# Attention with the values standing and Pool scaling the probabilities, and new orders at four borders of a two-layer trunk

## The reference, cut to what matters

```
for l in (0, 1):
    hn = rms_norm(x)                               # x: 256 tokens x 1024, float32
    qa, ka, va, cq, ckv, kr, gates = split(hn @ w_in[l])
    # branch A: 8 heads of 64, q and k normed and rotated, causal softmax
    # branch B: 8 heads, q = rms_norm(cq) @ w_uq, (k, v) = rms_norm(ckv) @ w_ukv,
    #           q and k of 96 per head, v of 64, normed and rotated, causal softmax
    y  = softmax(q k^T * scale + mask) v           # per head, both branches
    x += (sigmoid(g_a) * (ya @ w_br_a) + sigmoid(g_b) * (yb @ w_br_b)) @ w_out
    h  = rms_norm(x)
    x += swiglu(h) if l == 0 else the two best of 8 swiglu experts per token
```

## Time and profile before

| | |
|---|---|
| Median of 3 runs | 1358.72 us (1358.40 to 1359.19) |
| The profiled execution's own time | 1360.55 us |
| Its span | 1358.7 us |
| Mean granted clock of PE | 0.995 |
| PE busy | 1340.4 us, 99% |
| DVE busy | 1036.9 us, 76% |
| ACT busy | 891.0 us, 66% |
| POOL busy | 84.6 us, 6% |
| DMA, mean | 281 GB/s |

### The profile page before, as it was taken

The page is one execution under the profiler, slowest core; times in us unless marked ns, Lnnn a source line. Parts: engine busy times, 40 slices in busy tenths (PEclk is TensorE's granted clock), DMA queues, the critical chain, the costliest instruction groups (busy, mean ns, idle before and its releaser), DMA issues.

```text
span 1358.7 us, 17852 instructions
## 1 busy us (share of the span) xinstructions
PE 1340.4 (99%) x6433; PEld 1114.4 (82%) x6433; DVE 1036.9 (76%) x946; ACT 891.0 (66%) x931; POOL 84.6 (6%) x67
## 2 busy tenths in 40 slices
PE   9999999999999999999999999999999999999997
PEld 7878888888888788888888888888888888888885
DVE  5786665544467866679899898898898998988984
ACT  6675745444365766457787687787776876877773
POOL 1220000000003200000000000000000000000000
PEclk9999999999999999989999999999999999999999
DMA  7633446555456334679999999999999999999992
GB/s 269 215 94 125 155 160 215 184 188 175 150 162 220 120 116 148 243 277 391 367 361 383 367 379 390 368 383 391 375 382 388 365 382 368 382 393 360 383 391 63
DMA packets 172905, 381.22 MB, mean 281 GB/s; under 512 B 9098, under 2 KB 29236, under 8 KB 172852
## 3 DMA queue, kind: packets, MB, share of 16 engines
q1 hardware_dynamic: 169760, 369.95, 75.5%
q0 software_dynamic: 2304, 8.39, 2.4%
q10 hardware_dynamic: 788, 2.18, 0.4%
HBM read 374.20 MB, written 6.29 MB: 280 GB/s over the span
## 4 chain that ended last, share of the span: by engine, by line
PE 91%; DVE 4%; ACT 3%; issue 1%; DMA 1%; DVEq 0%; POOLq 0%; ACTq 0%
PE ps L1122 18%; PE ps L1124 18%; PE ps L1123 18%; PE ps L692 10%; PE ps L694 10%; PE ps L693 10%; PE ps L1188 1%; ACT w_hi L1307 1%; DMA raw<-in_w_in_dram 1%; ACT mix L1297 1%; DVE w_lo L1674 1%; PE ps L1203 1%; PE ps L811 1%; DVE mix L1709 1%; DVE mix L1712 1%
## 5 line engine op out<-in xcount | busy, mean ns | idle before, releaser
L1924 DVE TENSOR_TENSOR w_lo<-mix,w_hi 128x2048 fp32r<-128x2048 f32 (+1 forms) x192 | 408.2, 2150 | 68.0 <-ACT w_hi L1528 66.4
L1528 ACT CAST w_hi<-mix 128x2048 fp32r<-128x2048 f32 (+1 forms) x190 | 341.0, 1810 | 90.1 <-PE ps L1124 90.1
L1674 DVE TENSOR_TENSOR w_lo<-raw,w_hi 128x2048 fp32r<-128x2048 f32 (+3 forms) x94 | 198.5, 2118 | 108.8 <-ACT w_hi L1307 108.1
L1122 PE MATMUL ps<-w_hi,eT_hi 128*128 128x512 f32 x704 | 278.9, 396 | 1.6 <-DVE eT_lo L2058 1.6
L1124 PE MATMUL ps<-w_hi,eT_lo 128*128 128x512 f32 x704 | 274.4, 390 | 0.0
L1123 PE MATMUL ps<-w_lo,eT_hi 128*128 128x512 f32 x704 | 274.4, 390 | 0.0
L1307 ACT CAST w_hi<-raw 128x2048 fp32r<-128x2048 f32 (+3 forms) x94 | 166.4, 1777 | 139.8 <-PE ps L694 116.8
L1924 DVE TENSOR_TENSOR w_lo<-raw,w_hi 128x2048 fp32r<-128x2048 f32 (+1 forms) x96 | 193.2, 2032 | 17.0 <-ACT w_hi L1528 16.1
L1528 ACT CAST w_hi<-raw 128x2048 fp32r<-128x2048 f32 (+1 forms) x96 | 163.3, 1711 | 48.1 <-PE ps L1124 44.4
L692 PE MATMUL ps<-w_hi,hT_hi 128*128 128x512 f32 (+1 forms) x464 | 180.2, 388 | 2.0 <-DVE w_lo L1674 2.0
L694 PE MATMUL ps<-w_hi,hT_lo 128*128 128x512 f32 (+1 forms) x464 | 177.2, 382 | 0.0
(11 more groups left out here) (208 smaller groups left out, 1520.4 us busy)
## 6 DMA issues: line engine op xcount, KB each, us to landing
mix<-in_expert_w_gate_up_dram SPq DMA_DIRECT2D x111, 1024.0 KB, 10.4
raw<-in_expert_w_gate_up_dram SPq DMA_DIRECT2D x49, 1024.0 KB, 9.1
mix<-in_expert_w_down_dram SPq DMA_DIRECT2D x48, 1024.0 KB, 11.4
raw<-in_w_in_dram SPq DMA_DIRECT2D x28, 1024.0 KB, 5.3
raw<-in_expert_w_down_dram SPq DMA_DIRECT2D x24, 1024.0 KB, 13.2
raw<-in_dense_w_gate_up_dram SPq DMA_DIRECT2D x20, 1024.0 KB, 5.1
mix<-in_expert_w_down_dram SPq DMA_DIRECT2D x25, 512.0 KB, 7.8
raw<-in_dense_w_down_dram SPq DMA_DIRECT2D x9, 1024.0 KB, 4.8
```

Of the source, the lines that this page charges most:

```text
L1122: pe.matmul(out_, l_hi, w_hi[q][:, cols], start=first, stop=False, skip_group_check=True)
L1528: act.copy(w_hi[q][:, 0:m], e_raw[raw_of(p, first)][:, 0:m]).then_inc(e_hi_ready, 1)
L1674: dve.tensor_tensor(w_lo[q][:, 0:m], raw[u % RAW][:, 0:m], w_hi[q][:, 0:m].bitcast(F32), ALU.subtract).then_inc(split, 1)
L1924: dve.tensor_tensor(w_lo[q][:, 0:m], e_raw[raw_][:, 0:m], w_hi[q][:, 0:m].bitcast(F32), ALU.subtract).then_inc(e_split, 1)
```

## The change

It makes these changes:

- `values` is issued for two heads at every odd k. v stands in the array (64 columns) and the transposed probabilities move (256 columns for the first key tile, 128 for the second). The even head's result goes to partitions 0 to 63 and the odd head's to 64 to 127, so y comes out transposed. `turn_y` and `take_y` go. ACT and DVE make `yT` hi and lo from PSUM per four heads, hi at k = 4, 8, 12 and after the loop.
- The division by the row sum is now before the turning: Pool raises the two row sums to the power -1 and multiplies the probabilities in place (`scale_probs`), and `turn_probs` waits for it. Heads 0 to 2 come before Pool's last head scales, the others after.
- ACT's weight splits in the loop move from odd k to even k, behind `turn_b`'s copy; DVE's seventh `lo` stays, its fifth moves from score 13 to score 12.
- Start: the gain vector of the attention norm is loaded by Pool's queue and no more by ACT's; `hT` is split in two halves, and the first weight unit too, so that PE starts on the first half.
- ACT splits unit u0 + 15 after the copies of the transposed q and k.
- Dense end: DVE adds the first token tile's result to x in halves, the first one before its last `lo` of the stage.
- Routing: 8 filler products and no more 12 before the ranks, none and no more 14 after them; the gather goes to four banks in four groups; ACT's fourth expert split comes after the gather's scaling.

The diff, cut to its core:

```diff
             for t_, lo, hi in ... (low, PE)
-                        if t == 0:
+                        if t == 0 and u:
                             ready(u)
-                        for t_, lo, hi in ((cq, 0, Q_RANK), (ckv, Q_RANK, LOW)):
-                            for kk in range(2):
+                        for kk in range(2):
+                            if t == 0 and u == 0:
+                                pe.wait_ge((first_split, split)[kk], 1)
+                            for t_, lo, hi in ((cq, 0, Q_RANK), (ckv, Q_RANK, LOW)):
...
                 def turn_probs(k):
-                    pe.wait_ge(exp_done, 16 * l + k + 1)
+                    pe.wait_ge(probs_scaled, 16 * l + k + 1)
...
                 def values(k):
-                    vv = v[:, k // HEADS, :, (k % HEADS) * A_DIM:(k % HEADS + 1) * A_DIM]
-                    pe.matmul(bank[:, o0:o0 + A_DIM], pT[:, k % 2, 0:P], vv[:, 0, :], start=True, stop=True)
-                    pe.matmul(bank[:, o1:o1 + A_DIM], pT[:, k % 2, P:2 * P], vv[:, 0, :], start=True, stop=False)
-                    last = pe.matmul(bank[:, o1:o1 + A_DIM], pT[:, k % 2, 2 * P:3 * P], vv[:, 1, :], start=False, stop=True)
+                    def of(hd):
+                        rows_ = slice(hd % 2 * A_DIM, (hd % 2 + 1) * A_DIM)
+                        vv = v[:, hd // HEADS, :, (hd % HEADS) * A_DIM:(hd % HEADS + 1) * A_DIM]
+                        return ps[t_.bank][rows_, (hd // 2 % 2) * T:(hd // 2 % 2 + 1) * T], vv
+                    for hd in heads:
+                        out_, vv = of(hd)
+                        pe.matmul(out_, vv[:, 0, :], pT[:, hd % 2, 0:2 * P], start=True, stop=False, skip_group_check=True)
+                    for hd in heads:
+                        out_, vv = of(hd)
+                        last = pe.matmul(out_[:, P:T], vv[:, 1, :], pT[:, hd % 2, 2 * P:3 * P], start=False, stop=True,
+                                         skip_group_check=True)
...
-                    values(k)
-                    if k == 12:
-                        turn_y(0)
+                    if k % 2:
+                        values(k)
                 branch(0, 0, 0)
-                turn_y(1)
...
-                for _ in range(12):
+                for _ in range(8):
                     pe.matmul(ps[1][:, 0:2 * P], before, both, start=True, stop=True)
...
-                for _ in range(14):
-                    pe.matmul(ps[1][:, 0:2 * P], before, both, start=True, stop=True)
...
             ACT, mixer
-                    hi(u0 + 14 + half)
+                    if half == 0:
+                        hi(u0 + 14)
                 for hp in range(4):
                     copy_out(qkT_a[:, hp, :], t_, ps[t_.bank][:, :])
+                hi(u0 + 15)
...
-                    if k % 2:
-                        g = k // 2
-                        if g < 7:
-                            hi(u0 + 17 + g)
                     if k in B_TURNS:
                         copy_out(qkT_b[0:B_DIM, hd, :], t_, ps[t_.bank][0:B_DIM, :])
-                    if k == 12:
-                        turned_y(l, 0)
+                    if k and k % 2 == 0:
+                        hi(u0 + 16 + k // 2)
+                    if k and k % 4 == 0:
+                        turned_y(l, k // 4 - 1)
...
             DVE, mixer
-                splits = {5: 16, 7: 17, 9: 18, 11: 19, 13: 20, 14: 21, 15: 22}
+                splits = {5: 16, 7: 17, 9: 18, 11: 19, 12: 20, 14: 21, 15: 22}
                     if k >= 6 and (k - 6) % 4 == 0:
-                        take_y((k - 6) // 4)
-                take_y(3)
+                        yT_low((k - 6) // 4)
                 lo(u0 + 23)
-                yT_low(1)
+                yT_low(3)
                 lo(u0 + 24)
...
             DVE, dense
+                    if u == U["dn", FF - 1, 0] - 1:
+                        add_to_x(0, "dense", halves=(0,))
                     lo(u + SPLIT)
...
             Pool
+            pool.dma_start(gcol_first, a["attn_norm"].rearrange("l (r c) -> (l r) c", c=P)).then_inc(first_gain_in, 16)
...
+                def scale_probs(k):
+                    pool.wait_ge(exp_done, 16 * l + k + 1)
+                    b, hd = k // HEADS, k % HEADS
+                    pool.tensor_tensor(row_inv[:, b, :, hd], row_sum[:, b, :, hd], minus_one[:, :], ALU.pow).then_inc(inv_ready, 1)
+                    pool.wait_ge(inv_ready, 16 * l + k + 1)
+                    for t, (lo, hi) in enumerate(((0, P), (P, 3 * P))):
+                        p_ = pr[:, k % 2, lo:hi]
+                        last = pool.tensor_scalar(p_, p_, row_inv[:, b, t, hd:hd + 1], None, ALU.mult)
+                    last.then_inc(probs_scaled, 1)
                 for w in range(4):
+                    if w == 3:
+                        for k in range(3):
+                            scale_probs(k)
...
+                for k in range(3, 16):
+                    scale_probs(k)
```

More of the change, by code:

```diff
@@ L251, in plan_mixer @@
             if k % 4 == 0:
-                tile["y", l, k // 4] = banks.use(6 + k // 4 % 2)
-            if k == 12:
-                for j in range(2):
-                    tile["yT", l, 0, j] = banks.turns(4)
-        for j in range(2):
-            tile["yT", l, 1, j] = banks.turns(4)
+                tile["yT", l, k // 8, k // 4 % 2] = banks.use(6 + k // 4 % 2)
         for half in range(2):
@@ L1268, in _ @@
             gather_first()
-            for b in range(6):
+            for b in range(4):
                 pe.wait_ge(drained[b], bank_done[b])
@@ L1578, in gathered_first @@
             def gathered_first():
[L1579 to L1584 removed]
+                for g in range(4):
+                    act.wait_ge(gath_done if g % 2 else first_rows, g // 2 + 1)
+                    for m in range(2):
+                        kt = 2 * g + m
+                        last = act.mul(eT[0][:, kt, :], ps[4 + g][:, m * CAP:(m + 1) * CAP], gain(DEPTH - 1, "ffn", kt))
+                    last.then_inc(gath_hi if g % 2 else first_rows_hi, 1)
             def silu_e(i, j, first):
@@ L1933, in _ @@
             dve.wait_ge(gcol_set, 1)
-            hT_low(0, 0)
-            lo(0)
+            hT_low(0, 0, (0,))
+            for part_, ready_, done in ((slice(0, LOW), first_hi_ready, first_split), (slice(LOW, 2 * LOW), hi_ready, split)):
+                dve.wait_ge(ready_, 1)
+                dve.tensor_tensor(w_lo[0][:, part_], raw[0][:, part_], w_hi[0][:, part_].bitcast(F32), ALU.subtract).then_inc(done, 1)
             lo(1)
+            hT_low(0, 0, (1,))
             dve.wait_ge(gcol_turned, 2)
@@ L1958, in _ @@
             dense()
-            add_to_x(0, "dense")
+            add_to_x(0, "dense", halves=(1,))
             hT_low(2, 0)
```

129 lines of the change are left out of this document (54 added, 75 removed).

## The result

| | before | after |
|---|---|---|
| Median | 1358.95 us (4 runs, 1358.40 to 1359.70) | 1390.83 us (4 runs, 1389.99 to 1393.59) |
| Profiled execution: its own time, span | 1360.55, 1358.7 | 1393.59, 1391.8 |
| Mean granted clock of PE | 0.995 | 0.984 |

The changed kernel is slower: ratio 1.0237, 95% interval 1.0223 to 1.0252, +31.9 us. The forecast was 1364.4, +5.7.

What follows compares the result with a forecast made beforehand. PE, busy 99% of the span, was taken as the bound. Attention +10.0 (waits 11.3 less gains 6.3 a layer), start -1.9, dense end -0.9, routing -1.5: +5.7, forecast 1364.4 us (chance 0.40), range 1346 to 1371.

Steps and rivals of the forecast that it cites:

- Pool's two products: Pool's scaling of probabilities, 128 and 256 columns: 0.6 us a head, from two copies of 256 that took 0.74.
- New waits: PE's turnings of probabilities waiting for Pool, held up by DVE's subtractions: 11.3 us lost a layer, ends 3 and 15.
- Head 0: First head of a layer: Pool starts only after DVE's subtraction, so PE waits 2.7 us at its turning.
- Rival 3: A wait of 2.7 at head 0 may lower PE's clock in both layers: +9.1, 1367.8 us; chance 0.05.
- Values on the column halves: Value products of two heads run together on PE: 0.87 us a pair for 1.24, gaining 3.0 a layer.
- Turning of y: Sixteen PE transposes a layer go, eight having taken 0.88: gain 1.8 us a layer.
- kv border: First key-value product: ACT empties the query-key banks before splitting a weight unit, so PE's wait goes: gain 0.7 us.
- Start: PE's first product comes 1.9 us earlier with half units; gain vector by Pool's queue taken as 0, ends -0.2 and +1.
- Dense end: PE's 0.94 wait for the sum into x goes, as its first half moves ahead: gain 0.9 us.
- Routing: Fillers and a weight split leave around the gather: up to 2.4 us, taken as 1.5 because of the clock.
- Shifts whole: The experts' stage runs behind PE and moves as one, its loads being all in before it starts.
- upper bound for the waits: Upper end of PE's new waits, 15 us a layer, if Pool also loses every turn between DVE's back-to-back multiplies.

Runs made afterwards that it cites:

- e8: The changed kernel with the four products of a pair of values reordered, both of the even head, then both of the odd head; one execution, 1392.68 us.
- e7: The kernel before plus the four border changes, but the first gain vector loaded on ACT's queue as before the change; 1357.05 us, ratio 0.9978 to the kernel before.

## Why the prediction was wrong

Its sign was right, and so was its mechanism, a Pool held up by DVE between exponential and turning; a term of the sum failed, one rival came true beside the forecast, and one loss was in no case.

- **Pool's two products, the step that failed.** Taken as 0.6 from two copies of 256 columns. Copies in the same place took 0.63, the products 1.51, of which the 128 columns are 0.61. An operation was priced by another one. That 0.9 a head is worth 19.8 us (+8.0 to +27.8) of the 26.2 by which +31.9 misses +5.7, since at 4.4 us the chain has no room left in PE's head for a hold-up; the lower clock that the longer waits bring is in it.
- **New waits, 11.3 a layer.** Measured 31.6 in both, 15.8 a layer. With copies, which is what was priced, 17.8 in both, 8.9 a layer. Head 0: forecast 2.7, measured 3.36. There the prediction also read a row wrongly: it called the gap ahead of ACT's exponential its table load, "which does not move". The profile has ACT wait there for DVE's row maximum (1.49), and the exponential did move, to an end at 77.41 from 79.17, as much as the scores (1.76); the power then met a subtraction that had started with it. They do lie behind heads 4, 12 and 13 (1.40, 1.61, 1.61 in layer 0) and at head 3 (1.05, for 2.0 forecast), but the longest of the loop behind head 9 (2.51) and none behind 10, and at five more turnings that the prediction left free or held small: a late turning makes the next one late.
- **Rival 3, the clock, 0.05.** Came true as well. After the 3.36 of wait the 512-column products run at 0.43 from start to start instead of 0.23, until 86.4, and again from 89.6 to 93. In layer 0 the granted clock is 0.91 in the mean from 80 to 120 us and 0.96 from 120 to 160, together up to 5.2 us (9% and 4% of 40); in both layers it is about 12, where the rival had 3.4. It should have been part of the forecast: the wait that the prediction computed for head 0 (2.7) was longer than the one that had lowered the clock at the start (2.0).
- **Values on the column halves.** 0.87 a pair forecast, 0.80 measured (94.12 to 94.92). Right, and the order of the four products does not matter (0.81). So the rule cited from the Trainium skill (TensorE: Matmul & The Clock Gate, "Part 3: Packing small matmuls"), by which matmuls start and end in program order, does not hold between halves here: in that order 640 columns would have followed each other in e8 where 384 did, and e8's rows have the starts out of program order.
- **Turning of y, kv border.** 1.8 a layer forecast; at layer 0's branch products its second half is seen as 0.86. Border: 0.7 forecast, 0.88 measured. Without Pool's step, attention behind that border gained 5.0 in layer 0 and 4.4 in layer 1, for 5.6 forecast (3.0 + 1.8 + 0.8).
- **Start, 1.9.** 0.87 measured. The gain vector through Pool's queue held PE up for 1.9 (L1251) and came 1.0 later than before, the end that was given for it; the warm-up products behind it ran at the lower clock and stood in front of the first product (13.03). And the claim that the rest moves up is wrong: with the load on ACT's queue, PE waits for the fourth unit instead (e7).
- **Dense end, 0.9.** 1.1 measured, no wait left.
- **Routing, 1.5.** 2.7 measured in this trace, 1.1 to 2.9 over all. The gather did run partly at the lower clock (5.41 for 3.74), but the experts started 5.18 behind its start, for 5.39 before: its scaling in four groups hid it.
- **Experts.** "Shifts whole" was wrong by 5.3 us of span, 4.9 of them at the very end, in the gap behind PE's loop. No row of before points at it, and its cause is open.
- **The range**, 1346 to 1371: its upper bound for the waits (15 a layer) took Pool's products at 0.6 as well. The same row that gave the middle gave both ends, so neither covered it.

What stays open: how the waits divide between the chain's length and Pool's hold-ups by DVE. Both count: two heads ahead gives back 21 us with the hold-ups left in, and 17.2 us of waits remain. No run takes the hold-ups away and leaves Pool's chain as it is.

## What to carry to other kernels

Before an engine is put into a chain exponential, scaling, turning, copy, next exponential, add up that chain, add the longest hold-up that the new step can meet, and compare it with the bounding engine's work per step. As long as both fit, the step costs little (0.7 us of Pool: 2.7 us in 32 heads); once they don't, most of each further us is paid (0.6 a head, 20 us in 32 heads, cost 20.3; 0.9 a head, 28 us, cost 19.8). Price an operation by a row of that operation on that engine; if the trace has none, the unknown price belongs into the range with a factor of at least two. Waits of this size also bring the lower clock, about 12 us beside 31.6 of waits here. And when a kernel changes by some instructions only, look at the end of loops: a 4 us gap there may be nothing that the change means.

## What the runs showed of the hardware that I had not expected

- Pool multiplied 128 and 256 columns by a number per partition in 1.51 (0.61 of it for the 128), and copied both in 0.63; DVE took 0.55 for both products, and 0.16 for the reciprocal for which Pool's power took 0.72.
- PE's four products of a pair on the two column halves took 0.80 in one order and 0.81 in the other, with starts that are not in program order.
- The place of PE's instructions moved about 4 us: the same columns at the start as 48 products and not 12 took away a gap of 2.5 us, and the lower clock behind it, 1370 us later. An instruction DMA lies there with and without the gap.
- DVE was hardly held up by Pool in the one place looked at: a product of DVE at 100.10 took 1.97 instead of 1.76 while Pool's product ran from 99.41 to 100.92, while Pool waited for DVE by up to 2.3.
